# An expert stage with a third set of weight places, one loop over groups, and states loaded at its end

## What is computed

```python
g_idx = jnp.argmax(group_score, axis=-1)                 # best of 4 groups of experts
_, local = lax.top_k(in_group, TOP_K)                    # then 2 experts in it
for e in range(N_EXPERTS):
    hid = jax.nn.silu(xt @ wg[e]) * (xt @ wu[e])         # 1024 -> 512, twice
    y = y + gates[:, e:e + 1] * (hid @ wd[e])            # 512 -> 1024
```

## Time and profile before

| | |
|---|---|
| median of three runs | 1430.92 us |
| the profiled execution | 1430.51 us, of which the trace's span is 1428.3 us |
| granted clock, mean | 0.846 |
| busy: PE, DVE, ACT, POOL | 1075.3, 413.6, 152.5, 236.2 us |
| layer 0's expert stage on TensorE | 322.6 to 596.1 us |
| layer 1's expert stage on TensorE | 1123.8 to 1394.3 us |

### The profile page before, as it was taken

The page is one execution under the profiler, slowest core; times in us unless marked ns, Lnnn a source line. Parts: engine busy times, 40 slices in busy tenths (PEclk is TensorE's granted clock), DMA queues, the critical chain, the costliest instruction groups (busy, mean ns, idle before and its releaser), DMA issues.

```text
span 1428.3 us, 21314 instructions
## 1 busy us (share of the span) xinstructions
PE 1075.3 (75%) x8508; PEld 596.0 (42%) x8509; DVE 413.6 (29%) x849; ACT 152.5 (11%) x313; POOL 236.2 (17%) x356
## 2 busy tenths in 40 slices
PE   5995666926489887459999999999895355589870
PEld 4643343413255454234354554544444233245540
DVE  0499543440001110152232433324126000001105
ACT  1012232101001000011101111011001000001000
POOL 1394100120111211101112212111000200111210
PEclk9996666957789999869999999999996677799985
DMA  9601370446999987762553626524225487999873
GB/s 339 231 1 50 111 294 30 153 158 255 410 414 421 422 350 315 284 205 91 189 192 122 212 94 210 194 95 178 89 118 189 165 335 325 372 404 415 341 292 113
DMA packets 81194, 327.68 MB, mean 229 GB/s; under 512 B 7107, under 2 KB 16415, under 8 KB 72805
## 3 DMA queue, kind: packets, MB, share of 16 engines
q1 hardware_dynamic: 59469, 259.70, 46.3%
q0 software_dynamic: 16048, 50.69, 10.3%
q10 hardware_dynamic: 5616, 16.42, 3.3%
HBM read 297.20 MB, written 32.59 MB: 231 GB/s over the span
## 4 chain that ended last, share of the span: by engine, by line
PE 56%; DMA 23%; DVE 13%; issue 3%; POOL 2%; ACT 1%; SPq 1%; ACTq 0%; POOLq 0%; DVEq 0%
DMA ring<-in_w_e_up_dram 16%; PE ps L1651 12%; PE ps L1573 11%; DVE scratch L1308 5%; PE ps L1598 4%; DMA ring<-in_w_e_down_dram 4%; PE ps L1870 4%; PE ps L1970 4%; PE ps L1897 3%; PE ps L1689 2%; PE ps L1883 2%; PE ps L1835 2%; DMA ring<-in_w_in_a_dram 1%; PE ps L1888 1%; PE ps L1934 1%
## 5 line engine op out<-in xcount | busy, mean ns | idle before, releaser
L1573 PE MATMUL ps<-ring,scratch 128*32 128x256 f32 x3840 | 253.8, 425 | 128.2 <-DMA ring<-in_w_e_up_dram 114.2
L1573 PEld LDWEIGHTS ps<-ring,scratch 128*32 128x32 f32 x3840 | 149.3, 122 | 222.4 <-issue 171.9
L1651 PE MATMUL ps<-xT,ring 128*128 128x320 f32 x640 | 187.3, 454 | 3.7 <-DMA ring<-in_w_in_a_dram 2.9
L1651 PEld LDWEIGHTS ps<-xT,ring 128*128 128x128 f32 x640 | 127.0, 200 | 64.3 <-issue 19.6
L1598 PE MATMUL ps<-ring,scratch 128*32 128x256 f32 x1920 | 116.0, 390 | 22.9 <-DMA ring<-in_w_e_down_dram 14.7
L1217 DVE TENSOR_TENSOR scratch<-scratch,ps 64x512 f32<-64x512 f32 x30 | 20.6, 685 | 387.4 <-ACT scratch L837 387.4
L651 POOL DMA_INDIRECT y_quarters<-scratch x60 | 59.2, 987 | 351.9 <-DVE scratch L1223 342.8
L1598 PEld LDWEIGHTS ps<-ring,scratch 128*32 128x32 f32 x1920 | 62.2, 112 | 68.0 <-DMA ring<-in_w_e_down_dram 18.2
L1466 DVE SCALAR_TENSOR_TENSOR scratch<-scratch,ps 128x512 f32<-128x512 f32 x64 | 43.9, 687 | 136.4 <-PE ps L1897 129.3
L1308 DVE SCALAR_TENSOR_TENSOR scratch<-scratch 128x256 f32<-128x256 f32 x120 | 75.6, 705 | 0.0
L1870 PE MATMUL ps<-ring,xT 128*128 128x512 f32 x128 | 57.9, 605 | 0.0
(11 more groups left out here) (298 smaller groups left out, 1044.7 us busy)
## 6 DMA issues: line engine op xcount, KB each, us to landing
ring<-in_w_e_gate_dram SPq DMA_DIRECT2D x32, 2048.0 KB, 13.0
ring<-in_w_e_up_dram SPq DMA_DIRECT2D x32, 2048.0 KB, 17.5
ring<-in_w_e_down_dram SPq DMA_DIRECT2D x32, 2048.0 KB, 16.2
scratch<-in_state_ret_dram POOLq DMA_DIRECT2D x32, 512.0 KB, 5.7
ring<-in_w_in_c_dram SPq DMA_DIRECT2D x8, 2048.0 KB, 13.3
out_ret_sample_dram<-scratch POOLq DMA_DIRECT2D x32, 512.0 KB, 4.4
ring<-in_w_in_a_dram SPq DMA_DIRECT2D x5, 2048.0 KB, 21.6
ring<-in_w_in_c_dram SPq DMA_DIRECT2D x8, 1024.0 KB, 12.0
```

Source lines behind the costliest of these rows:

```text
L1573: ins = pe.matmul(ps[r0:r0 + CHUNK, B_GU + hf, a2 * 256:a2 * 256 + 256], xgT[:, k, c0:c0 + CHUNK], ring[:, slot + j, k * D_FF + n * 256:k ...
L1651: ins = pe.matmul(bank(j)[:, 0:TOK], w[:, k, k0:k0 + P], xT[:, k, :], start=k == 0, stop=k == KD - 1)
```

## The change

* **Three sides.** A third set of three places, `more`, is cut out of `scratch` in the expert stage, where the mixers' buffers are dead by then; the layouts A, C and M are reordered for it. `slot(s)` gives the place. Expert e of layer l uses side (e + 2l) mod 3. `by_side` has three branches instead of two.
* **One loop.** TensorE's loop does a whole group per pass: gate and up of chunks 0, 1, 2, `turn_hidden`, gate and up of chunk 3, down of chunk 0, `turn_hidden`, `turn_rows` for the next group, down of chunks 1, 2, 3. Nothing stands ahead of it but the first `turn_rows`, and nothing behind it; the last pass turns the rows of one group more than there are, so the table gets an empty group (`TABLE_QUADS`). ScalarE, VectorE and GpSimd loop to match.
* **Loads.** SyncE loads experts 0, 1 and 2 before the plan (the new places as soon as the mixer's buffers are dead, in layer 1 when all states have been stored), and then, in straight code, gate, up and down of expert e in this order: gate when the gate and up products of expert e-3 are done, up at once, down when its down products are done. At the end of layer 0's stage the first three blocks of the next mixer are loaded before the results are fetched, and the next three after.
* **Moved.** The five states and `tbc` are loaded at the end of layer 0's expert stage.

The diff, cut to its core:

```diff
+TABLE_QUADS = MAX_QUADS + 1
+SLOTS = 9
+SLOT = 4096
...
+                  ("lngb", 2048), ("pad2", 686), ("more", 3 * SLOT), ("yy", 3 * 2 * D, "xg"))
+        def slot(s):
+            return ring[:, s, :] if s < RING else M["more"][:, (s - RING) * SLOT:(s - RING + 1) * SLOT]
...
+        def side_of(l, e):
+            return (e + 2 * l) % 3
...
-                gate_up_loads(l, 2, 0, 1)
-                with sp.Fori(1, N_EXP // 2 - 1) as i:
-                    gate_up_loads(l, i * 2 + 1, 1, i)
-                    down_load(l, i * 2, 0, i)
-                    gate_up_loads(l, i * 2 + 2, 0, i + 1)
-                    down_load(l, i * 2 + 1, 1, i)
...
+                for e in range(3, N_EXP):
+                    chunks = sp.value_load(done_i[0:1, e - 2:e - 1], min_val=1, max_val=MAX_CHUNKS + 1)
+                    for j in range(3):
+                        s = 3 * side_of(l, e) + j
+                        sp.wait_ge(e_landed[s], 16 * (earlier_turns(l, s // 3) + e // 3))
+                        if j != 1:
+                            sp.wait_ge(L[l]["y_full" if j == 2 else "gu_full"], chunks)
+                        load_expert(l, e, j)
...
+            experts(0, [(s, used(s)) for s in range(4)] + [(s, heads_turned) for s in (6, 7, 8)] + [(s, used(s)) for s in (4, 5)])
...
-            pool.wait_ge(S["x_done"], 3)
+            experts_pool(pool, 0)
             for j in range(S0_RING):
                 load_state(j)
-            experts_pool(pool, 0)
...
-                with pe.If(side == 0):
-                    products(0)
-                with pe.If(side == 1):
-                    products(3)
+                for e in range(3):
+                    with pe.If(side == e):
+                        products(3 * side_of(l, e), 16 * earlier_turns(l, side_of(l, e)))
...
-            gate_up(0, 0, experts_of(0)[0:2])
-            turn_hidden(0, 0)
-            with pe.Fori(0, last) as i:
-                six = experts_of(i)
-                gate_up(i, 1, six[2:4])
+            with pe.Fori(0, last + 1) as i:
+                four = experts_of(i)
+                gate_up(i, 0, 0, *four[0])
+                gate_up(i, 0, 1, *four[1])
+                gate_up(i, 1, 0, *four[2])
+                turn_hidden(i, 0)
+                gate_up(i, 1, 1, *four[3])
+                down(i, 0, 0, *four[0])
+                turn_hidden(i, 1)
                 turn_rows(i + 1)
-                down(i, 0, six[0:2])
-                turn_hidden(i, 1)
-                gate_up(i + 1, 0, six[4:6])
-                down(i, 1, six[2:4])
-                turn_hidden(i + 1, 0)
-            six = experts_of(last)
-            gate_up(last, 1, six[2:4])
-            down(last, 0, six[0:2])
-            turn_hidden(last, 1)
-            down(last, 1, six[2:4])
+                down(i, 0, 1, *four[1])
+                down(i, 1, 0, *four[2])
+                down(i, 1, 1, *four[3])
```

More of the change, by code:

```diff
@@ L352, in build, with earlier_turns @@
         w_landed = [sem(f"w_landed{s}") for s in range(RING)]
-        e_landed = [[sem(f"e_landed{l}_{s}") for s in range(RING)] for l in range(2)]
+        e_landed = [sem(f"e_landed{s}") for s in range(SLOTS)]
+        def side_of(l, e):
+            return (e + 2 * l) % 3
+        def earlier_turns(l, side):
+            return sum(side_of(0, e) == side for e in range(N_EXP)) if l else 0
         last_job = {}
@@ L368, in build @@
         loads, landed_at, last_in_slot = {}, [0] * RING, [{}, {}]
-        for l, (count, first) in enumerate(((7, 5), (16, 2))):
+        for l, (count, first) in enumerate(((7, 5), (16, 3))):
             for n in range(count):
@@ L509, in gate_up_loads @@
[L509 to L516, removed]
-            def down_load(l, e, side, turns):
-                chunks = sp.value_load(done_i[0:1, bass.ds(e - 1, 1)], min_val=1, max_val=MAX_CHUNKS + 1)
-                s = 3 * side + 2
-                sp.wait_ge(e_landed[l][s], turns * 16)
-                sp.wait_ge(L[l]["y_full"], chunks)
-                load_expert(l, e, 2, s)
@@ L526, in experts @@
[L526 to L539 removed]
+                    return gu[e].rearrange("(p k) f -> p (k f)", k=KD)
@@ L571, in _, with used, heads_turned @@
                 load_pages(g + 2)
-            experts(0)
+            def used(s):
+                return lambda: await_full(sp, last_in_slot[0][s])
+            def heads_turned():
+                for i in range(2):
+                    await_full(sp, ("aoT", i))
+                await_full(sp, ("cT", 2))
+            experts(0, [(s, used(s)) for s in range(4)] + [(s, heads_turned) for s in (6, 7, 8)] + [(s, used(s)) for s in (4, 5)])
             def load_c(n):
@@ L844, in experts_act @@
             turned(0)
-            swish(0, 0)
-            hidden(0, 0)
-            with act.Fori(0, last) as i:
-                swish(i, 1)
+            with act.Fori(0, last + 1) as i:
+                for hf in range(2):
+                    swish(i, hf)
+                    hidden(i, hf)
                 turned(i + 1)
-                hidden(i, 1)
-                swish(i + 1, 0)
-                hidden(i + 1, 0)
-            swish(last, 1)
-            hidden(last, 1)
+            act.wait_ge(Q["xa_done"], last + 2)
+            act.sem_inc(S["met"], 1)
             act.wait_ge(Q["y_out0"], last * 32 + 32)
@@ L1199, in experts_dve @@
                 link(dve.scalar_tensor_tensor(code, at_place[u], float(N_EXP ** u), code, ALU.mult, ALU.add))
-            for u in range(2):
-                link(dve.scalar_tensor_tensor(code[:, 0:MAX_QUADS - 1], at_place[u][:, 1:MAX_QUADS], float(N_EXP ** (4 + u)),
-                                              code[:, 0:MAX_QUADS - 1], ALU.mult, ALU.add))
             dve.tensor_copy(experts_i, code)
@@ L1230, in experts_dve @@
             turned(0)
-            hidden(0, 0)
-            with dve.Fori(0, last) as i:
+            with dve.Fori(0, last + 1) as i:
+                hidden(i, 0)
                 hidden(i, 1)
@@ L1235, in experts_dve @@
                 result(i, 0)
-                hidden(i + 1, 0)
                 result(i, 1)
-            hidden(last, 1)
-            result(last, 0)
-            result(last, 1)
             for t in range(3):
```

180 lines of the change are left out of this document (93 added, 87 removed).

## The result

The changed kernel takes 1648.76 us (median of 4 runs, 1641.79 to 1654.48) against 1425.87 us of the kernel before (4 runs beside them): a ratio of 1.156, 95% interval 1.148 to 1.165. Its profiled execution spans 1640.0 us, 211.7 us more than before. The prediction said 1568 us and 1360 to 1625: slower, by the mechanism it named, but 81 us too little and outside its range.

The account below looks back on a forecast made before the run. Expert stages were taken as partly bound by weight loading, then by instruction fetches. Layer 0 +88.9, layer 1 +46.6 and states +2 made 137.5 us on the 1428.3 us span; with 2.2 us outside it, 1568 us, range 1360 to 1625.

Parts of the forecast that it names:

- The body is fetched anew in every pass: TensorE's expert loops: ten packets fetched each pass, layer 0 +88.9 us, layer 1 +46.6 us; chance 0.52.
- The premise beside it: TensorE's instruction memory: eight packets is all that is known to have been held at once; the new body exceeds it.
- The price of a packet: TensorE's instruction fetches: 2.0 us a packet, kept between 0.63 and 2.37; ten packets cost 20 us a pass.
- A group's own time: Expert stages: TensorE by itself needs 25.3 us a group, making a pass 45.3 us with fetches.
- Waits for weights: TensorE in the expert stages: the third side gives back at most 54.7 us in layer 0, 74.1 in layer 1.
- Order inside the pass: TensorE's loop: `turn_hidden`'s waits are covered by products; taken as nothing, about 1 us a pass if not.
- States at the stage's end: End of layer 0's stage: the moved states share the DMA engines with the results, charged at 2 us.
- the holes of rows 9: Behind layer 0's loop: TensorE's "issue" stalls of 2.00, 2.17, 2.37 and 0.26 us at four packets.
- that rival: Second mixer's start: results and states queue behind weight blocks, adding some 25 us to any case; chance 0.05.
- The fast rival: Expert stages: body stays (1344 us) or fetches are hidden (1363 us at 0.63 us a packet); chance 0.26.
- Part of the body stays: TensorE's loop: only some packets, say six of ten, are fetched each pass; 1448 us, chance 0.22.

Follow-up runs that it names:

- e1: The kernel before with a never-taken third branch at all eight choices of TensorE's loop; 1652.1 us, ratio 1.163.
- e3: The changed kernel with a third place for the down weights alone, two for gate and up; 1573.6 us, ratio 1.109.
- e2: The changed kernel with two places instead of three, so two branches per choice; 1534.3 us, ratio 1.078.
- e10: The kernel before with 64 instructions that only count a semaphore at TensorE's start; 1514.3 us, ratio 1.061.
- e8: The changed kernel with only waits in its branches, products standing once and reading residual rows as weights; layer 0's stage 238.9 us, total not comparable.
- e5: e2 with 102 instructions that only count a semaphore at TensorE's start; 1537.2 us, ratio 1.081.
- e4: The kernel before with a never-taken third branch only at the loop's four choices of gate and up; 1619.2 us, ratio 1.143.
- e6: The kernel before with 154 instructions that only count a semaphore at TensorE's start; 1507.0 us, ratio 1.060.
- e7: The changed kernel with each stage as two loops, gate and up then down, plus 64 idle instructions at TensorE's start; 1435.2 us, ratio 1.013.
- e9: e7 with two waits taken out of its order, in the first loop's hidden transposes and the second loop's result buffers; 1399.8 us, ratio 0.980.

## Where the prediction was right, and where its sum failed

*The body is fetched anew in every pass.* Right: 86 and 75 packets where ten a pass, some eighty, were forecast, and e1 shows that nothing else is needed for the loss. The premise beside it was too generous: two of the eight packets seen were counted for the code ahead of the loop, and the loop itself lies in seven, borders shared. Loops in seven stayed, e3's in eight did not. The Trainium skill (Runtime: NRT & Kernel Launch, section Instruction fetch mechanics) gives TensorE's instruction memory as 2048 instructions; e2's layer 1 and e10's loops, of some 1650 records, were fetched nevertheless. Why seven is the most that stayed, no run shows.

*The price of a packet.* Right in its sum, by two small misses that cancel: 20.0 us a pass were charged, and "issue" took 162.3 / 8 = 20.3 us and 131.6 / 7 = 18.8 us. The stalls are uneven (2.3 to 3.7 us, and 9.07 at the jump back), and 10.7 packets come at 1.75 to 1.9 us instead of ten at 2.0. The reason given for 2.0, no more than a microsecond of matmuls in hand, is borne out by the trace before: when the packets of the three full stalls started, at 574.96, 580.87 and 586.79 us, TensorE had 0.9, 0.6 and 0.9 us of matmuls left. With the other waits TensorE stood still for (408.8 - 246.6) / 8 = 20.3 us and (357.4 - 218.2) / 7 = 19.9 us a pass.

*A group's own time.* This is the term that failed. 25.3 us were taken from a piece of the loop that ran without long waits, and the text expected "a granted clock that stays high". Measured were 246.6 / 8 = 30.8 us and 218.2 / 7 = 31.2 us of busy time a pass, as the clock was granted at 0.79 and 0.78 in the stages where it had been 0.90 and 0.83. With 31.0 us a pass is 51.0: layer 0 +134.5, layer 1 +86.5, and with the other terms 1653 us. The profile before had the sign of it. Its last block behind the loop, after three holes of 2 us, took 5.11 us for 59 matmuls where 64 take 3.66, at a granted clock of 0.70; the two blocks before it still ran at 1.00. The first 64 of each stage, behind long waits, took 5.78 and 6.26 us. And layer 1's stage, with its long waits, already took 188.0 / 7 = 26.9 us of busy time a group. I read the holes of rows 9 for the price and not the lengths beside them. The range failed with it: its high end varied the price of a packet and held the group's time fixed.

*Waits for weights.* Right: all but gone. *Order inside the pass*, taken as nothing: `turn_hidden` (L1589) waits in the changed kernel's stages for nothing but 2.1 and 0.8 us of "issue", so no cost shows here. With two places, the new order and its loads make layer 0's stage 12 us longer (e2). *States at the stage's end*, charged at 2 us: nothing. Asked and first used, as in the earlier trace rows:

```profile
738.24 3.04 ACTq L870 DMA_DIRECT2D scratch<-y_quarters  x6
...
742.84 1.23 DVE L1247 SCALAR_TENSOR_TENSOR x<-x,scratch 128x1024 f32<-128x1024 f32 x1 [8.93 <-DMA scratch<-y_quarters]
```

4.6 us lie between the two, as before; that rival falls. *Reading weights from the scratch* costs nothing either: gate and up matmuls average 482 ns from the ring and 476 ns from the scratch.

*The fast rival* was sound as far as loading goes: 227 us worked out for layer 0, 239 in e8. It failed on its condition, 0.9 us a packet: a packet cost twice that. *Part of the body stays* happens, but only in some passes of loops that touch eight packets (e5, e10), not of one that touches ten.

*What no term held:* the stretch between the stages is 12.2 us shorter (last section), which hid part of the miss: 46.4 + 40.3 us of longer passes, less 14.2 us here against the 2 charged, plus 1.7 at the start, make the 74.2 us by which the span exceeds the forecast.

## What to carry to other kernels

A branch costs its code even when it isn't taken: before a loop on TensorE is given more branches, count its records and the packets that they touch where they lie, and read q8 in the middle of the stage, before and after. Where a stall of any kind is charged, charge the slower matmuls behind it too: in the profile the length of the first block after a hole says how much. And a new place for data paid here only where the code that reads it stayed loaded: splitting a loop in two, so that each part fits, gave 2% where one long loop lost 16%.

## What had not been expected of the hardware

Whether a loop of 6.5 packets stays depends on where it begins. The same code took 286 or 348 us in layer 0 and 369 or 312 us in layer 1 (e2, e5), and 64 idle instructions at the start of the kernel before cost 6.1% (e10).

The second mixer, with the same work, took less time behind a stage that stalled: 511.9 to 516.0 us between the stages in the seven kernels whose layer 0 was fetched (the changed one, e1, e3, e4, e5, e6, e10), and 519.8 to 528.7 us in the four complete kernels where it wasn't (before, e2, e7, e9). The clock alone doesn't account for it. TensorE was busy in that stretch for 461 us at a granted clock of 0.89 in the kernel before and in e2, and for 446 to 450 us at 0.90 to 0.91 in all the others, with e7 and e9 among them, whose layer 0 was not fetched. e8, not fetched either and without the experts' work, has 517.9 us. What sets the clock there stays open.
